# Strided columns of the stationary operand in the FFN's down projection, and a two-part moving operand in one block

## What is computed

```
def swiglu(h, w_g, w_u, w_d):
    return (jax.nn.silu(h @ w_g) * (h @ w_u)) @ w_d
...
x = x + g2 * swiglu(modulate(rms_norm(x, norm2_w[i]), sh2, sc2),
                    w_ffn_gate[i], w_ffn_up[i], w_ffn_down[i])
```

## Time and profile before

| | |
|---|---|
| median of three runs | 2597.87 us |
| the profiled execution's own time | 2595.86 us |
| its span | 2594.1 us |
| TensorE busy in matmuls / in weight loads | 2583.6 / 2131.0 us |
| VectorE / ScalarE busy | 1839.9 / 1263.0 us |

### The profile page before, as it was taken

One profiled execution on the slowest core, in us unless ns is written; L12 is line 12 of the kernel. 1 busy time (PEld: TensorE's weight loads), 2 busy tenths in 40 slices (PEclk: granted clock), 3 DMA queues, 4 the chain that ended last, 5 costly groups with the idle time before them and its releaser, 6 DMA issues.

```text
span 2594.1 us, 29936 instructions
## 1 busy us (share of the span) xinstructions
PE 2583.6 (100%) x11760; PEld 2131.0 (82%) x11760; DVE 1839.9 (71%) x2238; ACT 1263.0 (49%) x1584; POOL 33.3 (1%) x37
## 2 busy tenths in 40 slices
PE   9999999999999999999999999999999999999999
PEld 7888878888887888888888878888788888888887
DVE  6888868888886886567766666677656666655557
ACT  6455544645554467544555544444544444444443
POOL 0000000000000000010000000000000000000000
PEclk9999999999999999999999999999999999999999
DMA  8855567575657767777666667777467777655554
GB/s 329 277 206 207 185 231 259 199 266 204 208 195 268 267 219 256 256 258 252 235 216 219 222 225 258 258 248 242 169 229 238 239 238 240 224 191 206 191 189 160
DMA packets 163997, 595.30 MB, mean 229 GB/s; under 512 B 18097, under 2 KB 18257, under 8 KB 162449
## 3 DMA queue, kind: packets, MB, share of 16 engines
q1 hardware_dynamic: 158352, 571.41, 64.9%
q0 software_dynamic: 2416, 11.93, 1.3%
q10 hardware_dynamic: 3088, 10.04, 1.1%
HBM read 591.20 MB, written 2.11 MB: 229 GB/s over the span
## 4 chain that ended last, share of the span: by engine, by line
PE 98%; DVE 2%; ACT 0%; DMA 0%; issue 0%; POOL 0%; SPq 0%; DVEq 0%; ACTq 0%
PE ps L852 31%; PE ps L854 31%; PE ps L853 31%; PE ps L876 1%; PE ps L944 1%; PE ps L1134 1%; PE ps L1047 1%; DVE w_lo L1270 0%; PE ps L960 0%; PE ps L970 0%; PE ps L979 0%; PE ps L1128 0%; PE ps L969 0%; PE ps L1164 0%; DMA raw<-weights 0%; PE ps L1108 0%
## 5 line engine op out<-in xcount | busy, mean ns | idle before, releaser
L1270 DVE TENSOR_TENSOR w_lo<-raw,w_hi 128x1024 fp32r<-128x1024 f32 x879 | 1073.6, 1224 | 698.1 <-ACT w_hi L476 696.2
L476 ACT ACTIVATE w_hi<-raw 128x1024 fp32r<-128x1024 f32 x879 | 930.7, 1060 | 1289.0 <-PE ps L854 1212.5
L852 PE MATMUL ps<-w_hi,act_hi 128*128 128x512 f32 x3104 | 1225.1, 395 | 3.2 <-DVE w_lo L1270 1.5
L854 PE MATMUL ps<-w_hi,act_lo 128*128 128x512 f32 x3104 | 1209.6, 390 | 0.0
L853 PE MATMUL ps<-w_lo,act_hi 128*128 128x512 f32 x3104 | 1208.2, 389 | 0.0
L852 PEld LDWEIGHTS ps<-w_hi,act_hi 128*128 128x128 f32 x3104 | 583.0, 188 | 125.5 <-issue 7.0
L854 PEld LDWEIGHTS ps<-w_hi,act_lo 128*128 128x128 f32 x3104 | 582.6, 188 | 122.8
L853 PEld LDWEIGHTS ps<-w_lo,act_hi 128*128 128x128 f32 x3104 | 583.3, 188 | 118.3 <-issue 1.0
L1288 DVE SCALAR_TENSOR_TENSOR raw<-raw,c_row 128x1024 f32<-128x1024 f32 x192 | 233.9, 1218 | 0.0
L852 PE MATMUL ps<-w_hi,br_hi 128*128 128x512 f32 x416 | 162.6, 391 | 0.0
L853 PE MATMUL ps<-w_lo,br_hi 128*128 128x512 f32 x416 | 161.9, 389 | 0.0
(11 more groups left out here) (272 smaller groups left out, 1121.6 us busy)
## 6 DMA issues: line engine op xcount, KB each, us to landing
raw<-weights SPq DMA_DIRECT2D x887, 512.0 KB, 4.2
raw<-mods SPq DMA_DIRECT2D x192, 512.0 KB, 4.5
flat<-ln_gb POOLq DMA_DIRECT2D x4, 1024.0 KB, 7.6
flat<-x_cols SPq DMA_DIRECT2D x8, 256.0 KB, 6.6
flat<-conv_pw POOLq DMA_DIRECT2D x8, 256.0 KB, 4.7
x<-x_in ACTq DMA_DIRECT2D x4, 512.0 KB, 5.6
flat<-ctx_in ACTq DMA_DIRECT2D x1, 2048.0 KB, 12.3
shared<-na_rows POOLq DMA_DIRECT2D x2, 1024.0 KB, 9.2
```

The source lines that it names most:

```text
L476: nc.scalar.activation(tiles_of(n)[0], raw[:, e % RAW, :], ACT.Copy).then_inc(hi_ready, 1)
L852: nc.tensor.matmul(acc, xh, wh, start=first, stop=False)
L854: mm = nc.tensor.matmul(acc, xl, wh, start=False, stop=last)
L1270: nc.vector.tensor_tensor(lo, raw[:, ENTRY[False, n] % RAW, :], hi.bitcast(F32), ALU.subtract).then_inc(lo_ready, 1)
```

## The change

Three things.

1. **Strided columns.** The down projection of blocks 0 to 9 (`form="strided"`) reads `br_hi` and `br_lo` through the view `by_position`, in which the four tiles lie innermost: value (tile k, position t) is at 4t + k. The 128 columns of a stationary piece are then four values, 16 bytes, apart. `hidden_hi` and `hidden_lo` write and read the two tensors through the same view. The three mixers before the FFN and the last block are as they were.
2. **Halves.** In FFN block 3 the gate and up matmuls name their moving operand as two parts of 256 columns. The bytes and their order are the same.
3. **Sixteen matmuls at the end of TensorE's program**, whose results nobody reads: four with 96 stationary columns, four with 64, and eight on 64 of the 128 rows, in banks 0 and 1.

```diff
+FF_FORMS = {3: "halves"}
...
+        def by_position(v):
+
+            return v[:, :, :].rearrange("p k t -> p (k t)").rearrange("p (t k) -> p t k", k=4)
...
-                            hidden_hi(f - 1, br_hi[:, :, :])
+                            hidden_hi(f - 1, by_position(br_hi).rearrange("p t k -> p k t"))
...
-            def products(hi, lo, kt, b, first, last, wh, wl, ts):
+            def products(hi, lo, kt, b, first, last, wh, wl, ts, form=None):
+                if form == "halves":
+                    wh, wl = (v.rearrange("p (b c) -> p b c", b=2) for v in (wh, wl))
                 for t in ts:
-                    xh, xl = hi[:, kt, t * P:(t + 1) * P], lo[:, kt, t * P:(t + 1) * P]
+                    if form == "strided":
+                        xh, xl = (by_position(v)[:, t * P:(t + 1) * P, kt] for v in (hi, lo))
+                    else:
+                        xh, xl = hi[:, kt, t * P:(t + 1) * P], lo[:, kt, t * P:(t + 1) * P]
...
-                chunk(q, of_group(s % 2, 4 if n % 2 else 6, 2, *((act_hi, act_lo) if f == FF - 1 else (br_hi, br_lo))))
+                last = f == FF - 1
+                chunk(q, of_group(s % 2, 4 if n % 2 else 6, 2, *((act_hi, act_lo) if last else (br_hi, br_lo))),
+                      form=None if last else "strided")
...
-                        chunk(q, of_group(s % 8, 2 if s < 8 else 0))
+                        chunk(q, of_group(s % 8, 2 if s < 8 else 0), form=FF_FORMS.get(f))
...
+            for cols in (96, 64):
+                for i in range(4):
+                    nc.tensor.matmul(bank(0)[0:cols, :], act_hi[:, 8 + i, 0:cols], w_hi[:, i, 0:COLS], start=True, stop=True)
+            for i in range(4):
+                for r in range(2):
+                    rows = slice(64 * r, 64 * r + 64)
+                    nc.tensor.matmul(bank(r), act_hi[rows, 8 + i, 0:P], w_hi[rows, i, 0:COLS], start=True, stop=True)
...
-                        hidden_lo(f - 1, br_hi[:, :, :], br_lo[:, :, :])
+                        hidden_lo(f - 1, *(by_position(v).rearrange("p t k -> p k t") for v in (br_hi, br_lo)))
```

More of the change, by code:

```diff
@@ L855, in products, with chunk @@
                 return mm
-            def chunk(n, tiles, ts=range(TT), count=chunk_used):
+            def chunk(n, tiles, ts=range(TT), count=chunk_used, form=None):
                 pe.wait_ge(lo_ready, n + 1)
@@ L861, in chunk @@
                     wh, wl = (v[:, u * COLS:(u + 1) * COLS] for v in w)
-                    mm = products(*tile, wh, wl, ts)
+                    mm = products(*tile, wh, wl, ts, form)
                 mm.then_inc(count, 1)
```

## The result

The changed kernel takes 2605.14 us (median of 8 runs, 2604.03 to 2606.06) against 2597.70 us for the kernel before (8 runs, 2596.47 to 2598.45): ratio 1.0029, 95% interval 1.0019 to 1.0038. It is 7.4 us slower. That lies in the stated range of 2594 to 2735, which was wide enough for most slower cases, but not in the forecast's own 2595 to 2603: the likeliest case was no change, and what came has the size of the small overrun, which had a chance of 0.08.

The account below looks back on a forecast made before the run. TensorE's own stream was taken to bound the kernel; strided loads, strided writes, halves and tail summed 0 + 0 + 0 + 0, giving 2598.0 us. The forecast's own range was 2595 to 2603, the whole range 2594 to 2735.

Parts of the forecast that it names:

- Halves: Block 3's 192 gate and up matmuls reading two runs: taken at 0, bounds -2.6 to +2.6 us.
- the small overrun: Rival, slower: strided loads end up at 230 to 265 ns from hand-overs; 2603 to 2635 us, chance 0.08.
- What bounds the kernel, and the count: TensorE's stream bounds it; 960 down-projection matmuls with 960 loads, each nanosecond of overrun costing 0.96 us.
- The strided load, taken at 0: Down-projection load of 128 strided columns: 219 to 232 ns against the 226.7 ns period, 0 to +5 us, taken as 0.
- the rate of 1.67 ns per 16-byte group: Moving operand's time per 16-byte group at 213.3 ns, applied to the load's 128 groups: 213 ns.
- the hand-over of 5 ns: What a contiguous load's 112 ns period has beyond 128 columns at 1.2 GHz (106.7), added to the strided load.
- the closing line: One number would make the forecast wrong: a strided load's occupancy; above 232 ns it fails.
- The rule on 16-byte lines: SBUF accesses going to another 16-byte line with every value pay a penalty of unstated size; it spoke against the change.
- The rival of a shared supply: Load and moving operand share one full supply: load 363 ns, +131 us, 2729; loads at 2692 to 2729 had chance 0.18.
- The copies: Strided writes of `hidden_hi` and `hidden_lo`: unchanged to fourfold time, slack 5.8 us, taken at 0; fourfold costs 3 us.
- The tail: Sixteen unread matmuls at the end: hidden with 0.56 us over even at 226.7 ns each; uncovered, 3.6 us.
- The chances: Within 0.2% 0.59, slower 0.38, faster 0.03; slower includes small overrun 0.08, 2692 to 2729 0.18, fourfold 0.09, evacuations 0.03.

## Why the prediction was right and wrong

*What bounds the kernel, and the count.* Right: TensorE's period times 960 is the loss. 8.3 ns x 960 = 8.0 us against 7.4 measured.

*The strided load, taken at 0.* This step failed. Its bracket of 219 to 232 ns, 0 to +5 us, came within 1 ns of the load's length (233 alone), and the choice inside it was wrong: by the length alone the cost would have been (233 - 226.7) x 960 = 6 us. But the reasoning under it failed deeper, in two places. The first is the rate of 1.67 ns per 16-byte group. It was read off the moving operand, which passes such a group in 0.90 ns when each value comes from a new one; that the load needs 1.8 was a near hit by accident. Nor does the hand-over of 5 ns show: the 4-apart loads of 128, 96 and 64 columns take 233.3, 177.5 and 119.6 ns, in proportion to their columns. The second is "the load may take 115 ns longer, a factor 2.02, before a matmul is late", and with it the closing line, that the forecast hangs on one number, the occupancy of a strided load. Both assume that load and matmul meet only at the end. The runs with 2-apart columns in the kernel (+6.1 us with a load of at most 118 ns) and with 96 columns 4 apart (5.4 ns over contiguous columns) show that a load under a matmul can delay that matmul.

*The small overrun.* Its size came, a load of 233 ns in its 230 to 265, and its reason did not: it spoke of hand-overs, and what came is a load at 1.8 ns a column and a delay of the matmul that lies over a load. That the time lies in the stated range is owed to the width of the range and not to this mechanism.

*The rule on 16-byte lines* (the Trainium skill, Advanced Engine Details and Errata, section SBUF Cachelines) is borne out for the load's own length: 110 to 112, 115 to 118 and 233 ns for 1, 2 and 4 values apart, that is nothing much while two columns share a line and 2.1 times as long when none do, just over the factor of two from which it becomes a loss. The 3-apart row fits too (253 ns, between 193 and 310). The rule says nothing of the delay at 2 apart, nor does it give a size.

*Two ports.* The rival of a shared supply was priced at +131 us and the Trainium skill (TensorE: Matmul & The Clock Gate, step 1) excludes it. The runs side with neither. A matmul is later with a strided load under it, by 7 ns at 2 apart, where the load's length can't be the reason, and never by 136; a shared supply that is full is excluded, and that a load leaves the running matmul alone is not borne out. Whether the two meet in their reads or elsewhere no run shows.

*The copies.* Right: 1.98 and 2.01 us, about twice and 1.6 times, hidden, and at 0 in the run with strided writes alone.

*Halves.* Right at 0: eleven blocks of them gave 2597.77 against 2597.77.

*The tail.* Right: hidden with 1.2 us over, as its last eight matmuls ran faster than assumed (eight in 1.2 us, not one per 226.7 ns).

*The chances.* The small overrun had 0.08 because only hand-overs spoke for it. With 8 ns of cover left of 115, a bracket that reached to 232 ns and a row that had never seen the two streams together, it should, by my judgement, have had as much as no change.

## What to carry to other kernels

Where weight loads run under matmuls, hidden does not mean free: the price of a load's access pattern is to be read from the period of the matmuls, not from the length of the load's row. Keep the stationary operand's columns next to each other where the matmul stream is the bound; here, with 128 columns, 8 and 24 values apart cost 8 to 12% of a 512-column matmul, and every other step tried above one cost 3 to 5%. And avoid a step in the moving operand: two values apart already doubled the matmul.

## What the runs showed of the hardware

- A load of 128 fp32r columns 4 values apart takes 231 to 233 ns, 1.8 ns a column at either level of the clock; a contiguous one 0.87 ns a column at 2.4 GHz and 1.67 (96 columns) at 1.2 GHz. 8 values apart it takes 241 ns.
- A moving operand with a step of 2, 3, 4 or 8 values takes 431 to 461 ns for 512 columns against 226.7.
- ScalarE writes 1024 fp32r values 16 bytes apart in 1.98 us against 1.02, 8 bytes apart (in the 2-apart kernel) in 1.07.
- Under a 512-column matmul the period rises from 226.7 ns to 230 with a contiguous load of 96 columns, to 230.8 with a contiguous one that starts two values further on, and to 233.3 with one 2 apart.
- What stays open: the rule by which a load delays the matmul over it. It is not the load's length alone, not a full bank, and for 2-apart columns not where the operands lie. Part of the 20 ns at 8 apart is the load's own length (241 ns). The loads 16, 24 and 32 apart were not run alone, and why these cost 9, 27 and 7 ns, and why 112 columns 2 apart cost 1 ns and 96 contiguous ones 3, no run here explains.
